# One constant in a memory layout: the inputs that TensorE streams start 448 instead of 320 bytes past the grid of the weights

## The reference, cut to what matters

```python
# first block
h = rmsnorm(x, norm_g)
v, bg, cg, za, u, zb, ga, gb = split(h @ w_in)                   # 2048 -> 14336
ya = (bg * causal_depthwise_conv(cg * v, conv_w) * silu(za)) @ w_out_a
yb = gelu(s5_scan(u, ...)); yb = yb * sigmoid(yb @ w_glu + b_glu)
yb = (yb * silu(zb)) @ w_out_b
x = rmsnorm(x + (sigmoid(ga) * ya + sigmoid(gb) * yb) @ w_o, final_g)
# second block
proj = rms_norm(x) @ w_in_2                                      # q, k, v and the inputs of rwkv7
mixed = concatenate([dilated_attention(q, k, v), rwkv7_time_mix(z)])
x = x + mixed @ w_out_2
gate, up = split(rms_norm(x) @ w_gate_up)                        # 2048 -> 2 * 5632
return rms_norm(x + (silu(gate) * up) @ w_down)
```

## Time and profile before

| | |
|---|---|
| time, median of 3 runs | 2258.92 us (2256.36 to 2259.85) |
| the profiled execution | 2257.79 us, span 2256.1 us |
| TensorE busy | 2211.6 us, 98% |
| VectorE busy | 1568.1 us, 70% |
| ScalarE busy | 1040.6 us, 46% |
| GpSimd busy | 264.4 us, 12% |
| DMA moved | 387.81 MB, 172 GB/s on average |
| mean granted TensorE clock | 0.996 of 2.4 GHz |

### The profile page before, as it was taken

The page is one execution under the profiler, slowest core; times in us unless marked ns, Lnnn a source line. Parts: engine busy times, 40 slices in busy tenths (PEclk is TensorE's granted clock), DMA queues, the critical chain, the costliest instruction groups (busy, mean ns, idle before and its releaser), DMA issues.

```text
span 2256.1 us, 51607 instructions
## 1 busy us (share of the span) xinstructions
PE 2211.6 (98%) x20556; PEld 2158.7 (96%) x20556; DVE 1568.1 (70%) x2060; ACT 1040.6 (46%) x1357; POOL 264.4 (12%) x178
## 2 busy tenths in 40 slices
PE   7999999999999999999999999899999999999997
PEld 7999999999999989999999888799999999999997
DVE  7789999889545667768766777676666666654444
ACT  6544444444544444556344444554444444444442
POOL 0344444444100000000011000000000000000000
PEclk9999999999999999999999999999999999999999
DMA  7555555555555555555555111255555555556554
GB/s 262 179 170 180 178 178 178 176 183 188 187 186 186 186 193 191 186 180 175 205 180 175 48 49 56 80 186 186 186 186 186 186 186 185 185 175 192 187 179 135
DMA packets 107104, 387.81 MB, mean 172 GB/s; under 512 B 12032, under 2 KB 12160, under 8 KB 106752
## 3 DMA queue, kind: packets, MB, share of 16 engines
q1 hardware_dynamic: 104400, 375.44, 51.0%
q0 software_dynamic: 2176, 9.78, 1.3%
q10 hardware_dynamic: 432, 1.21, 0.1%
HBM read 384.29 MB, written 2.10 MB: 171 GB/s over the span
## 4 chain that ended last, share of the span: by engine, by line
PE 92%; DVE 4%; ACT 2%; issue 1%; DMA 0%; DVEq 0%; SPq 0%; ACTq 0%
PE ps_main L1690 28%; PE ps_main L1691 28%; PE ps_main L1692 27%; PE ps_aux L1918 2%; DVE w_lo L976 1%; PE ps_main L1918 1%; PE ps_main L1991 1%; ACT w_hi L495 1%; PE ps_aux L1939 1%; DMA w_raw<-wmain 0%; PE ps_main L1992 0%; PE ps_main L1993 0%; PE ps_aux L1759 0%; PE ps_aux L1747 0%; PE ps_aux L1836 0%
## 5 line engine op out<-in xcount | busy, mean ns | idle before, releaser
L976 DVE TENSOR_TENSOR w_lo<-w_raw,w_hi 128x1024 fp32r<-128x1024 f32 x718 | 917.0, 1294 | 458.7 <-ACT w_hi L495 453.5
L495 ACT ACTIVATE w_hi<-w_raw 128x1024 fp32r<-128x1024 f32 x718 | 747.6, 1047 | 739.0 <-PE ps_main L1692 725.6
L1690 PE MATMUL ps_main<-xs,w_hi 128*128 128x256 f32 x1664 | 467.9, 281 | 2.7 <-DVE w_lo L976 1.8
L1692 PE MATMUL ps_main<-xs,w_lo 128*128 128x256 f32 x1664 | 464.4, 279 | 0.0
L1691 PE MATMUL ps_main<-xs,w_hi 128*128 128x256 f32 x1664 | 464.3, 279 | 0.0
L1691 PE MATMUL ps_main<-x3s,w_hi 128*128 128x256 f32 x1408 | 394.2, 280 | 0.0
L1690 PE MATMUL ps_main<-x3s,w_hi 128*128 128x256 f32 x1408 | 393.0, 279 | 0.0
L1692 PE MATMUL ps_main<-x3s,w_lo 128*128 128x256 f32 x1408 | 392.9, 279 | 0.0
L1690 PEld LDWEIGHTS ps_main<-xs,w_hi 128*128 128x128 f32 x1664 | 312.2, 188 | 9.5 <-DVE w_lo L976 5.0
L1692 PEld LDWEIGHTS ps_main<-xs,w_lo 128*128 128x128 f32 x1664 | 312.8, 188 | 0.0
L1691 PEld LDWEIGHTS ps_main<-xs,w_hi 128*128 128x128 f32 x1664 | 311.4, 187 | 0.0
(11 more groups left out here) (420 smaller groups left out, 3766.3 us busy)
## 6 DMA issues: line engine op xcount, KB each, us to landing
w_raw<-wmain SPq DMA_DIRECT2D x622, 512.0 KB, 3.4
w_raw<-wdown SPq DMA_DIRECT2D x80, 512.0 KB, 3.7
w_raw<-wdown SPq DMA_DIRECT2D x16, 256.0 KB, 2.7
bias<-bias POOLq DMA_DIRECT2D x8, 384.0 KB, 3.6
x_res<-xt POOLq DMA_DIRECT2D x4, 512.0 KB, 7.0
out<-x_res SPq DMA_DIRECT2D x3, 512.0 KB, 2.8
x_first<-xt SPq DMA_DIRECT2D x2, 512.0 KB, 6.9
x_first<-xt ACTq DMA_DIRECT2D x2, 512.0 KB, 9.5
```

The lines of the kernel that those rows point to most:

```text
L495: nc.scalar.activation(whi[:, s, 0:width], raw[:, s, 0:width], ACT.Copy).then_inc(hi_ready, 1)
L976: V.tensor_tensor(wlo[:, s, 0:width], raw[:, s, 0:width], whi[:, s, 0:width].bitcast(F32), ALU.subtract)\
L1690: nc.tensor.matmul(out, whi[:, s, w], high[:, k, :], start=(first and kk == 0), stop=False)
L1692: ins = nc.tensor.matmul(out, wlo[:, s, w], high[:, k, :], start=False, stop=(last and kk == kbs - 1))
```

## The change

The start of `work` is moved up by 128 bytes, and with it each tile that `wk` places, whichever engine reads or writes it. The rings, the small tiles and `x_raw_l` stay where they are. No instruction, wait, loop or size is changed.

```diff
         rho = at("rho", small + 14 * K + 192, [STATE_TILES])
-        work = small + 14 * K + 320
+        work = small + 14 * K + 448
 
         def wk(name, kb, shape, dtype=F32):
             assert base + work + kb * K + 4 * int(np.prod(shape)) <= nc.sbuf_usable_end, name
             return at(name, work + int(kb * K), shape, dtype)
```

## The result

The changed kernel takes 2241.33 us (median of 7 runs, 2234.6 to 2246.91); the kernel before, run beside it, 2258.46 us (7 runs, 2254.83 to 2264.37). The ratio is 0.993, with a 95% interval of 0.9917 to 0.9942. It is faster by 0.7%, 17 us, a quarter of the 68 us forecast and clear of noise.

What follows compares the result with a forecast made beforehand. TensorE, busy 98% of the span, was taken as the bound: number of matmuls times their pitch. A 70 us gain less 2 us given back, DMA 0, made -68 us, from 2258 to 2190 us, range 2184 to 2305.

Steps and rivals of the forecast that it cites:

- The pitch sets the time, and two pitches exist at one place: TensorE: time is 16,992 matmuls times the distance between starts, 117.8 ns slow or 113.3 quick at the same addresses.
- Step 1: TensorE: 15,800 slow matmuls go from 117.8 to 113.3 ns at the new place, a gain of 70 us.
- part of the gain: Rival, chance 0.08: TensorE's pitch stays bistable with other odds; half the matmuls become quick, 35 us gained, 2224.
- The sentence at the end: Prediction fails at step 1 if the quick state belongs to how a stream is entered, not where it lies.
- slower: Rival, chance 0.27: all three matmuls of each trio stall as x_raw_l's do, 44 us lost, 2303.
- nothing happens: Rival, chance 0.31: only the address remainder to 128 bytes matters, so 320 and 448 are one case; 2258.9 us.
- Step 2: VectorE and ScalarE: some weight splits come late at the quick pitch in the scan, giving back 2 us.
- Step 3: DMA: the ring's loads come 4% more often, 57% busy becomes 59%; hidden, 0 us.
- The lower end of the range: 2184 us: the gain without the give-back and with 400 more matmuls that gain.
- the give-back: The 2 us of step 2, expected as TensorE idle time before L1690, released by the weights' split.

Runs made afterwards that it cites:

- 64: Streamed inputs 64 bytes past the grid of the weights, against 320 in the kernel before: 2257.13 us, ratio 0.9997.
- 192: Streamed inputs 192 bytes past the grid of the weights, against 320 in the kernel before: 2243.41 us, ratio 0.993; its profiled run took 2220.36.
- the best version: Changed kernel (448) plus eight small bf16 matmuls as breaks where long stretches begin, against the kernel before: 2206.6 us, ratio 0.9776.
- breaks at 320: Kernel before (320) plus eight small matmuls where long stretches begin: five runs 2229.4 to 2231.9 us, five 2257.7 to 2264.0; ratio 0.994.
- at 0: Streamed inputs 0 bytes past the grid of the weights, against 320 in the kernel before: 2296.27 us, ratio 1.0168.
- the eight places tried: Streamed inputs at 0, 64, 192, 320, 384, 416, 448 or 480 bytes past the grid of the weights: from 2241.3 us (448) to 2296.3 (0).
- The remainders 32 and 96: Streamed inputs at 416 and at 480, against 320 in the kernel before: 2275.75 us (one run) and 2269.68 us (ratio 1.0052).

## Why the prediction was wrong

Its direction was right, and its size was four times too large. The 2241 us lie inside the range, but between the cases that the range was made of.

- *The pitch sets the time, and two pitches exist at one place.* Right. The count of 16,992 matmuls holds for every version, and the 113.3 and 117.8 ns with their price of 4.45 ns at each of the places 64, 192, 320 and 448. The price gave the 2206 us of the best version ahead of time, and it fits the step between the two groups of runs with breaks at 320.
- *Step 1, all 15,800 slow matmuls become quick.* This is the step that failed. The prediction asked whether the new place has a pitch of its own. It has none: the place changes which entrances lead to the quick state, and a stream keeps what it got. 4,770 more matmuls are quick in place of 15,800, 21 us in place of 70. The three stretches without a break of 2,062, 574 and 6,286 matmuls were entered long and stayed long; with eight breaks in them they went quick, and 35 us more were there. The reason given, that at 448 the moving stream passes the weights early in the load, was a guess and is refuted: 192, where that meeting is 320/512 into the load, does the same as 448, and 64 the same as 320.
- *The rival "part of the gain"* (0.08, 2224) was the mechanism that came about, "the pitch stays bistable, with other odds". The sentence at the end, that the prediction fails if the quick state belongs to how a stream is entered, named it too. The earlier trace rows had hinted at it: stretches of one piece of code took either pitch by turns. By turns they also use the two pairs of ring slots, so the rows alone did not show one address with both pitches, as the prediction has it; the run with eight breaks at 320 does. That was a reason to put the chance on the odds at the entrances and not on the addresses.
- *The rival "slower"* had its row in x_raw_l, and the row was near for the place it stood for: at 0 the whole kernel is at 120.0 ns, 2296 us with 2303 worked out. That nearness is part luck. The row stood beside operands at 320; beside operands at 448 or 192 the same x_raw_l at 0 costs nothing over 117.8 ns from 33 us on, so it was not the price of a place by itself. The rival was wrong in carrying it over to 448 by nearness: the remainder to 128 bytes carries it, and 448 leaves the same as 320.
- *The rival "nothing happens"* rested on that remainder and had the class right: of the eight places tried, the four that leave 64 to 128 bytes are the only ones with the 113.3 ns. Within that class 320 and 448 still differ in odds.
- *Step 2, VectorE.* Right in place (the scan, the split of the weights) and too small: 2 us forecast. The quick matmuls of a turn are worth 1.8 to 1.9 us, and 1.0 came, so 0.9 us went in each of eight turns. That is 7 us, the difference between the 21 us of shorter pitch and the 13.9 us of span.
- *Step 3, DMA.* Right: 57% busy in 1550 to 1850 before, 60% at 192 where that window is quick.
- *Two small points.* The lower end of the range is worked out 2 us too low. The gain without the give-back and with 400 more matmuls is 70 + 1.8 = 72 us, and 2258 - 72 = 2186. And the earlier trace rows print 0.12 and 0.11 us where the prediction says 0.13 and 0.12; the starts in the trace are 0.128 and 0.117 us apart by turns, so that reading holds.

The Trainium skill, "TensorE: Matmul & The Clock Gate", Part 2, step 1, says that the weight load and the streamed operand have independent SBUF read ports and that loading the next weights does not take read bandwidth from the running matmul. This case disagrees on both sides of the pair. Between 0 and 320 only the place of the tiles made by `wk` changed, the time differs by 1.7%, and no other engine has a part in the pitch. And the load is held too: it lasts 188 ns in both states at 320, which the prediction took for agreement, but 192 ns at 0, and 192 ns for one load in three in the long state at 448. The measurement decides.

Left open: what in the memory or in TensorE has these periods, why a stall shows up as a steady addition to each matmul, what it is about an entrance that picks the state, and why the place of the operands beside x_raw_l changes its stall. The runs show states, odds and their dependence on the place. The cause of them was not measured.

## What to carry to other kernels

Where TensorE's records are back to back, read the pitch from starts in several stretches of the trace, and compare it between stretches of the same shape: two values mean a state that can be won, worth 4% of the stretch here. Try the start of the streamed operand at all remainders to 256 bytes relative to the weights (a constant in the layout), since a bad one costs 1.7% and looks in the profile like a fully busy engine. When the stretches are long, look at what stands at their entrances; a small matmul there can be worth some 80 times its cost (28 us for 0.34), and a run that differs by the price of one stretch may have entered it in the other state.

## What the runs showed of the hardware that was not expected

- The distance in SBUF between the moving operand and the weights changes the steady pitch of fp32r matmuls of 256 columns: 113.3 ns at best, 120.0 ns at worst, with the clock granted in full and the same whether the other engines work or not.
- The weight load feels it too: 188 ns at 320, 192 ns at 0.
- The 113.3 ns appeared only where the distance leaves 64 to 128 bytes (four places). How many of its matmuls are quick went with the remainder to 256 bytes: 64 and 320 are alike in two kinds of run, 192 and 448 in one. The remainders 32 and 96 were tried at one place each.
- At one place two pitches are stable (113.3 and 117.8 ns), at another three (117.3, 118.7 and 120.0 ns). A stream of 6,286 matmuls over 740 us did not leave its state by itself in any trace.
- Runs of one program can differ by it: 2230 or 2260 us with breaks at 320, 2220 or 2243 us at 192.
